# mLSTM values token-major, norm sums in one pass, small operands in PSUM, and four stages in another step order

## The reference, cut to what matters

```python
def _rms(x, w=None):
    y = xf * lax.rsqrt(jnp.mean(xf * xf, axis=-1, keepdims=True) + EPS)
# _diff_attention, 8 heads, 4 query blocks of 128, for each:
    s = einsum(q, k) * scale; p = softmax(where(mask, s, -inf))
    a = p[:, :, 0] - lam * p[:, :, 1]; outs.append(a @ v)
# _mem_attention: softmax over 256 memory rows; mq = _rms(mq, mem_q_norm)
# mixer_ab: gated_delta_rule (4 heads, chunks of 64) beside mlstm_chunkwise (4 heads)
    qkv = silu(causal_conv(pa[..., :A_CONV_CH], conv_w)); qa, ka = l2norm(...)
    vb = pbf[..., 2 * B_QK:2 * B_QK + B_V].reshape(b, s, B_HEADS, B_DV)   # mLSTM values
    num = inter * (q_ @ c_st) + pmat @ v_ ; hout = num / max(|den|, exp(-mt))
# mixer_c: sliding-window attention, 16 heads, with sinks
```

## Time and profile before

| | us |
|---|---|
| runs | 3319.86, 3320.51, 3324.14 |
| median | 3320.51 |
| the profiled execution | 3321.06 |
| its span | 3319.3 (1.76 less than its time) |
| PE busy | 3201.5 (96%) |
| DVE, ACT, POOL busy | 1198.9, 1244.8, 1741.9 |
| granted clock of PE, mean | 0.984 |

### The profile page before, as it was taken

The page is one execution under the profiler, slowest core; times in us unless marked ns, Lnnn a source line. Parts: engine busy times, 40 slices in busy tenths (PEclk is TensorE's granted clock), DMA queues, the critical chain, the costliest instruction groups (busy, mean ns, idle before and its releaser), DMA issues.

```text
span 3319.3 us, 40137 instructions
## 1 busy us (share of the span) xinstructions
PE 3201.5 (96%) x15014; PEld 2612.0 (79%) x15014; DVE 1198.9 (36%) x2174; ACT 1244.8 (38%) x2233; POOL 1741.9 (52%) x1351
## 2 busy tenths in 40 slices
...
GB/s 156 102 95 99 86 87 75 83 82 77 61 61 64 67 95 108 83 89 102 99 98 90 67 32 45 42 54 71 105 97 99 95 77 40 67 88 97 99 102 82
DMA packets 149839, 275.58 MB, mean 83 GB/s; under 512 B 16528, under 2 KB 17808, under 8 KB 149520
## 3 DMA queue, kind: packets, MB, share of 16 engines
...
## 4 chain that ended last, share of the span: by engine, by line
PE 86%; DVE 8%; POOL 3%; ACT 2%; issue 1%; DMA 0%; DVEq 0%; SPq 0%; ACTq 0%; POOLq 0%
PE PS L649 84%; PE PS L716 1%; POOL WL L2397 1%; POOL SM L2397 1%; DVE AR L1251 1%; DVE AL L1251 1%; DVE TMP L1257 1%; DVE TMP L1251 1%; ACT TMP L2013 1%; DVE SM L1251 1%; POOL TMP L2397 1%; DVE ACC L1257 0%; DVE SM L1257 0%; DVE AR L1257 0%; DVE X L1251 0%
## 5 line engine op out<-in xcount | busy, mean ns | idle before, releaser
L2397 POOL TENSOR_TENSOR WL<-RAW,WH 128x512 fp32r<-128x512 f32 x1002 | 1306.0, 1315 | 986.3 <-ACT WH L2013 985.8
L2013 ACT ACTIVATE WH<-RAW 128x512 fp32r<-128x512 f32 x1002 | 618.7, 627 | 1078.3 <-PE PS L649 1016.5
L649 PE MATMUL PS<-HH,WH 128*128 128x512 f32 x2296 | 917.9, 400 | 12.7 <-ACT WH L2013 8.0
L649 PE MATMUL PS<-HL,WH 128*128 128x512 f32 x2296 | 904.5, 394 | 2.7 <-DVE HL L1257 2.7
L649 PE MATMUL PS<-HH,WL 128*128 128x512 f32 x2296 | 903.5, 393 | 1.7 <-POOL WL L2397 1.7
L649 PE MATMUL PS<-AH,WH 128*128 128x512 f32 (+1 forms) x1504 | 585.4, 389 | 5.1 <-ACT AH L2013 3.5
L649 PE MATMUL PS<-AL,WH 128*128 128x512 f32 (+1 forms) x1504 | 583.1, 388 | 4.0 <-DVE AL L1251 3.2
L649 PE MATMUL PS<-AH,WL 128*128 128x512 f32 (+1 forms) x1504 | 581.2, 386 | 1.4 <-POOL WL L2397 1.4
L649 PEld LDWEIGHTS PS<-HH,WH 128*128 128x128 f32 x2296 | 437.4, 190 | 108.1 <-issue 9.6
L649 PEld LDWEIGHTS PS<-HL,WH 128*128 128x128 f32 x2296 | 437.4, 190 | 97.6 <-DVE HL L1257 7.6
L649 PEld LDWEIGHTS PS<-HH,WL 128*128 128x128 f32 x2296 | 436.2, 190 | 96.0 <-POOL WL L2397 3.3
...
## 6 DMA issues: line engine op xcount, KB each, us to landing
...
```

Of the source, the lines that this page charges most:

```text
L649: return e.matmul(o, l, r, start=a, stop=z, skip_group_check=True)
L2013: return e.activation(o, a, f, **kw)
L2397: return e.tensor_tensor(o, a, b, op)
```

## The change

Four edits.

1. The mLSTM's values: four `lin` of 24 matmuls of 512 columns, four DVE multiplies by RBT, and four times four transposes with an ACT copy go. In their place come two halves (two heads each) of eight `tok_row` steps, 12 matmuls of 256 columns each, into four banks, and for each half four ACT copies of 128x256 that multiply by the factor of `na`.
2. Twelve norms (`WHOLE`; `nr` counts four) have their last square gathered too, by POOL (`nfin`: DVE), and PE sums columns once.
3. Small operations go through PSUM: the variance is written to SBUF (for POOL) and to the norm's bank, the factor's products have one SBUF operand and one in the bank (`held`), and so the bank is held until the factor is made. The mLSTM's denominators and the window's maxima likewise. Two scalar_tensor_tensor become tensor_scalar.
4. The order: `DIFF`, `MEM`, `SWA` are new tables, `AB` is a table in place of the planner's order, and `LATE` is new.

```diff
+WHOLE = ("n1", "nmix", "nff", "nfin", "na", "nr", "nf0", "nc1", "nf1")
...
 DIFF = [
-    ("d_q", 1, 0), ("d_gain", 1), ("d_sm", 0, 0), ("d_sc", 0, 2), ("d_turn", 0, 0), ("d_sm", 0, 1), ("d_q", 1, 1), ("d_sc", 0, 3),
...
+    ("x", ("nt", 0)), ("d_sc", 1, 1), ("d_q", 2, 0), ("d_sm", 1, 0), ("d_t2", 0), ("d_gain", 2),
...
-PLAN = between(STEPS[0], ("d_q", 0, 0)) + DIFF + MEM + between(("f_up", 1, 0, 0, 0), ("e", 0, 0)) + SWA + between(("u", 1, 0, 0), None)
+PLAN = between(STEPS[0], ("d_q", 0, 0)) + DIFF + MEM + between(("f_up", 1, 0, 0, 0), ("ab_open", 0)) + AB + between(("u", 0, 0, 0), ("e", 0, 0)) + SWA + between(("u", 1, 0, 0), None)
 LATE = {
     "vector": {
+        ("d_rope", 2, 1): -4, ("d_sm", 0, 0): -2, ("d_sm", 1, 0): -2, ("d_sm", 2, 0): -2, ("d_sm", 3, 0): -2, ("d_sm", 4, 0): -2,
...
+        ("l", 2, 2, 2): 7, ("m_sc", 0, 1): 3, ("m_sc", 1, 1): 3, ("m_sc", 2, 1): 1, ("m_sc", 3, 1): 3, ("x", ("nk", 0)): 2,
...
     "gpsimd": {
-        ("bc", "nmem"): 1, ("mq", 7): 1, ("st", 9, 1): 2, ("ss", 0): -4, ("ss", 1): -4, ("ss", 3): -4, ("ss", 2): -4, ("ss", 4): -4,
...
+        m_value = lambda t: (tmp(4), tab(3))[t // 2][:, 256 * (t % 2):256 * (t % 2) + 256]
...
+        def last(n):
+            return NORM[n][2] - (1 if (n if isinstance(n, str) else n[0]) in WHOLE else 2)
...
-                    o = bank("var", n)
-                    e.wait_ge(*at("gathered_fin" if n == "nfin" else "gathered", n, K - 2))
-                    columns(o, 0, sq(n, 0), one1, True, NORM[n][3])
-                    e.wait_ge(*at("square", n, K - 1))
-                    columns(o, 0, sq(n, K - 1), one1, False, NORM[n][3]).then_inc(*up("mm", "fac", n))
+                    o = bank("factor", n)
+                    e.wait_ge(*at("gathered_fin" if n == "nfin" else "gathered", n, last(n)))
+                    z = columns(o, 0, sq(n, 0), one1, True, NORM[n][3])
...
+                elif kind == "m_v":
+                    p, k = i
+                    if k == 0:
+                        opened[kind] = [bank("m_v", p, t) for t in range(4)]
+                    tok_row(opened[kind], k, "w_in_ab_2", 0, BOFF + 1024 + 256 * p, 256, "H", k == 0, k == 7, ("m_v", p) if k == 7 else None)
...
-                tt(w[:, 2, :], w[:, 1, :], w[:, 1, :], MUL).then_inc(*up("root_squared", n))
-                e.wait_ge(*at("root_squared", n))
-                stt(w[:, 2, :], w[:, 2, :], -0.5 * post, w[:, 0, :], MUL, MUL).then_inc(*up("root_error", n))
+                e.wait_ge(*at("var_held", n))
+                tt(held(n, 2), held(n, 1), nwt(n, 1), MUL).then_inc(*up("root_once", n))
+                e.wait_ge(*at("root_once", n))
+                stt(held(n, 2), held(n, 2), -0.5 * post, nwt(n, 1), MUL, MUL).then_inc(*up("root_error", n))
...
-                elif kind == "m_vt":
-                    h = i[0]
-                    e.wait_ge(*at("mm", "m_vt", h))
-                    act(tab(3), psum("m_vt", h), ACT.Copy).then_inc(*up("m_vt", h))
+                elif kind == "m_v" and i[1] == 7:
+                    p = i[0]
+                    e.wait_ge(*at("mm", "m_v", p))
+                    e.wait_ge(*(at("mm", "m_num", 1) if p else at("factor", "na")))
+                    for t in range(4):
+                        act(m_value(t), psum("m_v", p, t)[:, 0:256], ACT.Copy, scale=nr("na")[:, t, 0:1]).then_inc(*up("m_v", p, t))
```

More of the change, by code:

```diff
@@ L284, in ml @@
     def ml(h, first=True):
-        return ([("m_v", h), ("m_q", h), ("m_k", h), ("m_og", h), ("m_vt", h)] if first else []) + [
+        return ([("m_q", h), ("m_k", h), ("m_og", h)] if first else []) + [
             ("m_w", h), ("m_sc", h, 0), ("m_sc", h, 1), ("m_sc", h, 2), ("m_sc", h, 3), ("m_nd", h), ("m_f", h), ("m_fin", h)]
@@ new lines @@
+    ("d_sc", 1, 2), ("d_sm", 1, 1), ("d_turn", 1, 0), ("d_q", 2, 1), ("d_sc", 1, 3), ("d_turn", 1, 1), ("d_sm", 1, 2), ("d_v", 2), ("d_f", 2),
+    ("x", ("nd", 2)), ("d_wide", 2), ("d_vt", 2), ("d_sm", 1, 3), ("d_turn", 1, 2), ("g", 0, 3), ("d_n", 2), ("d_turn", 1, 3), ("d_pv", 1),
+    ("r_out", 3, 3), ("d_rope", 2, 0), ("d_rope", 2, 1), ("d_add", 2, 0), ("d_add", 2, 1), ("g", 0, 4), ("d_sc", 2, 0), ("d_sc", 2, 1),
+    ("d_t1", 1), ("x", ("nt", 1)), ("d_q", 3, 0), ("d_gain", 3), ("d_sm", 2, 0), ("d_turn", 2, 0), ("d_sc", 2, 2), ("d_t2", 1), ("d_sm", 2, 1),
@@ new lines @@
+    ("d_q", 3, 1), ("d_sc", 2, 3), ("d_turn", 2, 1), ("d_sm", 2, 2), ("d_v", 3), ("d_f", 3), ("x", ("nd", 3)), ("d_vt", 3), ("r_out", 3, 4),
+    ("d_wide", 3), ("d_turn", 2, 2), ("d_sm", 2, 3), ("g", 0, 5), ("d_turn", 2, 3), ("d_n", 3), ("d_pv", 2), ("d_rope", 3, 0), ("d_add", 3, 0),
+    ("d_rope", 3, 1), ("d_add", 3, 1), ("r_out", 3, 5), ("d_sc", 3, 0), ("d_t1", 2), ("x", ("nt", 2)), ("d_sc", 3, 1), ("d_q", 4, 0),
+    ("d_gain", 4), ("d_sm", 3, 0), ("d_t2", 2), ("d_sc", 3, 2), ("d_turn", 3, 0), ("d_sm", 3, 1), ("d_q", 4, 1), ("d_sc", 3, 3), ("d_sm", 3, 2),
@@ new lines @@
+    ("d_turn", 3, 1), ("d_v", 4), ("d_f", 4), ("x", ("nd", 4)), ("d_wide", 4), ("d_vt", 4), ("d_sm", 3, 3), ("g", 0, 6), ("d_turn", 3, 2),
+    ("d_turn", 3, 3), ("d_n", 4), ("r_out", 3, 6), ("d_pv", 3), ("d_rope", 4, 0), ("d_add", 4, 0), ("d_rope", 4, 1), ("d_add", 4, 1), ("g", 0, 7),
+    ("d_sc", 4, 0), ("d_t1", 3), ("x", ("nt", 3)), ("d_sc", 4, 1), ("d_q", 5, 0), ("d_gain", 5), ("d_sm", 4, 0), ("d_t2", 3), ("d_sc", 4, 2),
+    ("d_turn", 4, 0), ("d_sm", 4, 1), ("d_sm", 4, 2), ("d_q", 5, 1), ("d_sc", 4, 3), ("d_turn", 4, 1), ("d_v", 5), ("d_f", 5), ("x", ("nd", 5)),
@@ new lines @@
+    ("d_turn", 4, 2), ("d_wide", 5), ("d_vt", 5), ("d_sm", 4, 3), ("g", 1, 0), ("d_turn", 4, 3), ("d_n", 5), ("d_pv", 4), ("d_rope", 5, 0),
+    ("r_out", 3, 7), ("d_add", 5, 0), ("d_rope", 5, 1), ("d_add", 5, 1), ("g", 1, 1), ("d_sc", 5, 0), ("d_t1", 4), ("x", ("nt", 4)),
+    ("d_sc", 5, 1), ("d_q", 6, 0), ("d_sm", 5, 0), ("d_sc", 5, 2), ("d_gain", 6), ("d_turn", 5, 0), ("d_sm", 5, 1), ("d_t2", 4), ("d_q", 6, 1),
+    ("d_sc", 5, 3), ("d_turn", 5, 1), ("d_sm", 5, 2), ("d_rope", 6, 0), ("d_add", 6, 0), ("d_v", 6), ("d_f", 6), ("d_turn", 5, 2),
```

233 lines of the change are left out of this document (125 added, 108 removed), and 88 rows, old and new, of tables (AB, LATE, MEM, SWA).

## The result

The changed kernel took 3272.99 us in the median (3267.63 to 3275.30, 4 runs) against 3321.24 for the kernel before (3319.86 to 3324.14, 4 runs). The ratio is 0.985, 95% interval 0.9837 to 0.9864. The forecast was 3252, range 3215 to 3300: the right side and inside the range, but 48 us of the 69 forecast. The profiled execution took 3272.71 us with a span of 3270.7, 48.6 less than before's span.

A forecast was written before the change was run, and what follows sets the result against it. PE was taken to bound the kernel: its own work, its idle time and a lowered clock. Terms -22 -6 -27 -4 -11 +2 = -68 took 3321 to 3253, less half a microsecond: 3252, range 3215 to 3300.

The forecast's parts named there:

- Differential attention: New order there: first turns -15.5, half clock -5, third turns -3, new wait at head 1's `d_pv` +1.5; -22 us.
- the first turns: In differential attention, PE's wait for DVE's probabilities at one place per head, eight in all, would go: 15.5 us.
- Small operations: Through PSUM, a chain of three takes up to 3 us less; counted only where PE waited, inside other terms.
- the -14: Delta stage's recursion: 18.6 us of waits and half clock, of which one root wait and its chain stay; -14 us.
- Memory attention: `nqm`'s sum waits less for POOL -2.5, half clock after it -2.5, reordered tail -1; -6 us.
- Delta and mLSTM: Stage's start -10, with a new wait of 3 at `gs`; recursion -14; rest -3; -27 us.
- The window: Sliding window: 3.5 us wait for `nc1`'s factor covered by `sv` 0, a half-clock piece gone; -4 us.
- Work: PE's work: twelve norms summed once -10.8, values +1.2 and -1.7, in all -11.3; later start of the sums +2 us.
- A: The forecast, waits go as said: 3252, own range 3232 to 3272; chance 0.5.
- B: Waits move rather than go, half of the 59 us of stalls coming back as new waits: 3282; chance 0.22.
- C: The clock recovers fully, no piece at half clock left in the four reordered stages: 3225; chance 0.18.
- E: Slower: norms' banks held until the factor is made, so PE waits for banks: 3328; chance 0.04.

The follow-up runs named there:

- combined: Changed kernel with differential attention's old table plus `d_sm` (h, 0) two places earlier, `n1` summed twice, roots of `nc1` and `nmem` earlier, `nqm`'s factor later: 3254.1 us.
- ab_plan: Changed kernel with the planner's order in the delta and mLSTM stage and without that stage's engine shifts: 3287.9 us, ratio 0.9893.
- values_only: Kernel before with the values' edit alone, the denominators and the window's maxima in PSUM coming with it: 3321.5 us, ratio 0.9996.
- small_sbuf: Changed kernel with the norms' factors computed in SBUF as before, the mLSTM's and the window's small operations staying in PSUM: 3279.4 us, ratio 0.9867.

## Why the prediction was right, and where it was off

The forecast was right in direction and range, and for most terms in mechanism. The waits came nearer to it than the clock did. Its 59 us of stalls were some 39 of waits and 20 of half clock; 27.7 and 9.7 came.

**Differential attention (-22, measured -14.0).** The mechanism of the first turns is right: alone, the shift gives 15.3 us of waits and 5.2 of clock, where 15.5 and 5 were put. The new wait at head 1's `d_pv` came too, 1.3 us where 1.5 was put. Two steps failed. "One new wait" was all that the sum held against the table, and the reading stopped at head 1; the new table's other seven heads are not copies of it. Head 4's last turn stands behind `x` and `d_wide` with little cover, head 7's lost the projection that covered it, and the table costs 10 us against the old one. And the term of 5 for half clock came out at 0.4: the three pieces of 3.4 us went, and 6.8 and 3.4 came behind the new waits.

**Small operations (part of -14 and -4).** Shown worth 5 us of waits, 4.2 of them in differential attention, where none was counted, 1.0 around the window, and none in the delta stage, where the -14 counted them.

**Memory attention (-6, measured -3.1 beside work).** The wait at `nqm` went whole, and a wait of 2.7 us came at `bc` `nmem`, whose root stood behind `nqm`'s of 2.9 us on POOL; half clock follows it, 3.4 us where 6.8 stood. The sum had no such wait in it. `combined` takes it away, and the stage is 2.3 us shorter.

**Delta and mLSTM (-27, measured -19.4 beside work).** The order takes 10.4 us of waits and the other edits none (`ab_plan`, `values_only`). The clock gave 8.8, where pieces worth 5.1, 5.1 and 3.4 were put in the sum. The statement that `gs` becomes a new wait is right where PE comes to it early (4.5 us in `values_only`, 4.0 in `combined`), and 0.9 in the change's own trace. That removing DVE's wait for `m_v` 0 is itself a gain is wrong: `values_only` shows none. The -14 also does not follow from its own parts: 18.6 less a root of 1.1 and three operations of 0.16 is 17, which would have put the forecast 3 us further off.

**The window (-4, measured -4.7).** Right in size, wrong in place: the 3.5 us wait that was to be covered stayed at 3.4, with 6.8 us of half clock behind it. Other waits of the stage shrank, by 2.6 us net. The size is luck.

**Work (-11, and +2).** The sums and values came out at -11.2, the recorded instructions at the prices of the earlier trace rows. What the later gathering gives back is 3 to 4 us, not 2: at the start not the sum but a WL panel stands behind POOL's addition.

**Rivals.** Of 59 us of stalls, 37 net went (48.6 less the 11.2 of work). That is between the forecast A and half-and-half, B: 3273 is 1 us outside A's own range of 3232 to 3272 and 9 short of B's 3282. B's reason, that a step put earlier puts another later, is what heads 4 and 7, `bc` `nmem` and `gs` show. The full recovery of the clock, C, did not come: the mean went from 0.984 to 0.987, where the forecast's signs had 0.99. The slower one, E, had no part: `small_sbuf` gives the norms' banks back early, and PE idles more there, 95.2 us against 90.1.
